# The x transposes of the expert two ahead, between up and the next gate

## The chip, the cores and the metric

The kernel runs on one core of a Trainium2 chip. The metric is the device time of one execution in microseconds. TensorE does the matmuls, VectorE and ScalarE take their results out of PSUM, GpSimd issues gathers, and SyncE issues the loads of the weights. Each engine works through its own queue in order, and semaphores are all that binds them.

## The reference

One step of a hybrid backbone over 128 context and 256 latent tokens, all in float32, with a model width of 1024: modulated norms, four token mixers, and then a mixture of 16 experts of width 512, two per token. The change lies in the last part alone:

```python
h = jax.nn.silu(jnp.einsum("td,edf->tef", t, w_gate)) * jnp.einsum("td,edf->tef", t, w_up)
h = h * gates.astype(h.dtype)[..., None]
return jnp.einsum("tef,efd->td", h, w_down).reshape(B, L, D)
```

## The kernel before

The expert stage takes experts one after another, in pairs (p is 0 or 1); all pairs but the first and the last run in a hardware loop. For each expert, GpSimd gathers its rows of the normed tokens (at most 96) into `xe`. TensorE turns them in eight transposes (`turn_x`, line 845, called by `load_x`) into PSUM banks 0 and 1, and ScalarE copies them to `xeT` (`xt_out`, line 1398). `gate` and `up` are eight terms each over 128 rows of contraction. They are packed: `packed` (lines 834 and 837) splits the array into four groups of 32 columns, of which three hold the 96 tokens' first 384 output columns and the fourth the other 128 for each of the three. A float32 term shows as two passes in the trace, each of three matmuls of 384 columns and three of 128, so `gate` is 16 passes, and `up` too. ScalarE applies silu to gate's result (`gate_silu`, line 1406, into `he`), and VectorE multiplies by up's (line 2011). TensorE transposes h (`turn_h`, three full transposes, line 851), VectorE copies these to `heT` (line 2015), and `down` multiplies by the third weight in the same packed form, again 16 passes. ScalarE and VectorE copy the two halves of the result and ScalarE's queue writes them out.

Nothing but the order of the code sets the order on an engine. TensorE's for expert n is: up of n; gate of n + 1; the h transposes of n; the x transposes of n + 2; down of n. The last pair has no x transposes. The weights lie in six slots, three for each parity; SyncE reloads a gate, up or down slot once that step of the expert in it is done, so each load is asked for nearly two expert steps before its use. The gather for expert n + 2 waits for the x transposes of expert n (`xt_filled`).

Of the kernel before, what the change touches and what calls it, by code (L numbers as in the profile page):

```python
# [154 lines left out]
def backbone_step(nc, cols, A, O):  # L155
# [10 lines left out]
    with ctx:  # L166
# [250 lines left out]
        def _(pe):  # L417
# [408 lines left out]
            n = len(uses)  # L826
# [3 lines left out]
            def packed(bank, x, w, terms):  # L830

                for k in range(terms):
                    for g in range(3):
                        mm(psum[32 * g:32 * g + 32, bank, 0:PACK], x(k, g), w(k)[:, 0:PACK], start=(k == 0),  # L834
                           stop=(k == terms - 1), tile_position=(0, 32 * g))
                    for g in range(3):
                        last = mm(psum[96:128, bank, tile(g)], x(k, g), w(k)[:, PACK:CW], start=(k == 0 and g == 0),  # L837
                                  stop=(k == terms - 1), skip_group_check=True, tile_position=(0, 96))
                return last

            def turn_x(src):

                for kt in range(KT):
                    c = kt % 4 * ROWS
                    last = tr(psum[:, kt // 4, c:c + ROWS], src[0:ROWS, tile(kt)], ident[0:ROWS, 0:ROWS])  # L845
                return last

            def turn_h(p):

                for q in range(3):  # L850
                    last = tr(psum[:, 4, tile(q)], he[:, p, tile(q)], ident)  # L851
                return last

            def up(p, bank, w):
                return packed(bank, lambda k, g: xeT[p][:, k, 32 * g:32 * g + 32], lambda k: w[:, k, :], KT)

            def down(half, w):
                return packed(5 + half, lambda q, g: heT[:, q, 32 * g:32 * g + 32] if q < 3 else heT[:, g, ROWS:P],
                              lambda q: w[:, q, half * CW:half * CW + CW], FE // P)

            def load_x(n, p, it):

                pe.wait_ge(s[f"xe{p}"], 16 * it + 16)
                turn_x(xe[p]).then_inc(s["xt_filled"], 1)

            def gate(n, p, it):

                pe.wait_ge(s["xt_ready"], n + 1)
                pe.wait_ge(loaded[NS * p], 16 * (it + (0 if p else PRE_USES)) + 16)
                up(p, 2, slot[NS * p]).then_inc(s["gate_done"], 1)  # L870

            def experts(it, first, last_pair):
                for p in range(2):
                    n = 2 * it + p
                    base = 0 if p else PRE_USES
                    pe.wait_ge(loaded[NS * p + 1], 16 * (it + base) + 16)
                    if not (first and p == 0):
                        pe.wait_ge(s["h_ready"], n)
                    up(p, 3, slot[NS * p + 1]).then_inc(s["up_done"], 1)
                    if not (last_pair and p == 1):  # L880
                        pe.wait_ge(s["g_silu"], n + 1)
                        gate(n + 1, 1 - p, it + p)
                    pe.wait_ge(s["h_ready"], n + 1)
                    if not (first and p == 0):
                        pe.wait_ge(s["ht_ready"], n)
                    turn_h(p).then_inc(s["ht_filled"], 1)
                    if not last_pair:
                        load_x(n + 2, p, it + 1)
                    w = slot[NS * p + 2][:, :, :].rearrange("p k n -> p (k n)").rearrange("p (k d) -> p k d", d=D)
                    pe.wait_ge(loaded[NS * p + 2], 16 * (it + base) + 16)  # L890
                    pe.wait_ge(s["ht_ready"], n + 1)
                    if not (first and p == 0):
                        pe.wait_ge(s["ya"], n)
                        pe.wait_ge(s["yb"], n)
                    down(0, w)
                    down(1, w).then_inc(s["down_done"], 1)
# [3 lines left out]
            load_x(1, 1, 0)  # L900
            gate(0, 0, 0)
            experts(0, True, False)
            with pe.Fori(1, E // 2 - 1) as it:
                experts(it, False, False)
            experts(E // 2 - 1, False, True)


# [227 lines left out]
        def _(act):  # L1135
# [249 lines left out]
            def write_rows(block, p, signal):  # L1385

                rows = A["y_rows"][block * ROWS:(block + 1) * ROWS, :] if isinstance(block, int) else \
                    A["y_rows"][bass.ds(block * ROWS, ROWS), :]
                act.dma_start(rows.rearrange("r (h c) -> r h c", h=2)[:, :, 0:PACK], yp[p][0:ROWS, :, :]
                              ).then_inc(signal, 16)  # L1390
                act.dma_start(rows.rearrange("(g r) (h c) -> r h g c", g=3, h=2)[:, :, :, PACK:CW],
                              yp[p][ROWS:P, :, :].rearrange("r h (g c) -> r h g c", g=3)).then_inc(signal, 16)

            def xt_out(n, p, reused):
                act.wait_ge(s["xt_filled"], n + 1)
                if reused:
                    act.wait_ge(s["up_done"], n - 1)
                a(xeTa[:, p].rearrange("p (b k) n -> p b (k n)", b=2), psum[:, 0:2, 0:KT // 2 * ROWS], ACT.Copy  # L1398
                  ).then_inc(s["xt_ready"], 1)

            def gate_silu(n, p, reused):

                act.wait_ge(s["gate_done"], n + 1)
                if reused:
                    act.wait_ge(s["ht_filled"], n - 1)
                a(he[:, p, 0:PACK], psum[:, 2, 0:PACK], ACT.Silu).then_inc(s["g_silu"], 1)  # L1406

            def experts(it, first, last_pair):
                for p in range(2):
                    n = 2 * it + p  # L1410
                    if not (last_pair and p == 1):
                        gate_silu(n + 1, 1 - p, not (first and p == 0))
                    if not last_pair:
                        xt_out(n + 2, p, True)
                    act.wait_ge(s["down_done"], n + 1)
                    if not first:
                        act.wait_ge(s[f"y_out{p}"], 32 * it)
                    a(yp[p][:, 0, :], psum[:, 5, 0:PACK], ACT.Copy).then_inc(s["ya"], 1)  # L1418
                    act.wait_ge(s["ya"], n + 1)
                    act.wait_ge(s["yb"], n + 1)  # L1420
                    write_rows(n, p, s[f"y_out{p}"])

            xt_out(0, 0, False)
            xt_out(1, 1, False)
            gate_silu(0, 0, False)
            experts(0, True, False)
            with act.Fori(1, E // 2 - 1) as it:
                experts(it, False, False)
            experts(E // 2 - 1, False, True)
            with act.If(further(act) > 0):  # L1430
                with act.Fori(0, OVER) as o:
# [655 lines left out]
```

## Time and profile before

| | us |
|---|---|
| median of 3 runs | 700.31 (699.57 to 706.39) |
| profiled execution, its own time | 701.97 |
| its span, first to last instruction | 700.0 |
| ten expert steps, 458.20 to 629.20 | 171.00 |
| TensorE busy in the span | 601.7 (86%) |

The expert stage begins at 385 us with the first x transposes and ends near 666 us. Mean granted clock of TensorE over the span is 0.939 of 2.4 GHz. A row of the timeline gives the start, the time from the first start to the last end of a group of like instructions, the engine and the line; PE is TensorE's matmuls and PEld its weight loads. Ends of matmuls are modelled.

### The profile page before, as it was taken

To read this page: it belongs to the slowest core of one execution; us is meant where nothing else is said; L and a number is where in the kernel's file an instruction comes from. 1 tells how busy PE (TensorE), PEld (TensorE's weight loads), DVE (VectorE), ACT (ScalarE), POOL (GpSimd) and SP (SyncE) were. 2 spreads that over 40 slices of the span, in tenths; PEclk is the share of its full clock that TensorE was granted. 3 is DMA by queue.
4 is the path that set the end of the run, shared out by engine and by line. 5 is a ranking of instruction groups with operands and counts; after the bars stand their busy time and mean duration, and the time that the engine had idled before them with its cause. 6 is when DMAs were issued, how large, how long until landed. Compare 5 with 4: busy or idle time off the path is not lost.

```text
span 700.0 us, 15233 instructions
## 1 busy us (share of the span) xinstructions
PE 601.7 (86%) x6792; PEld 473.6 (68%) x6792; DVE 252.2 (36%) x518; ACT 142.6 (20%) x254; POOL 61.3 (9%) x89
## 2 busy tenths in 40 slices
PE   2989999999998996799642999999999999999900
PEld 0665534666756565744342899999999999999800
DVE  2660768878648147110656300000000000011026
ACT  1421454322176110100240111111111111111012
POOL 1065000000110000200001100000000000200030
PEclk9999999999998999999875799999999999999965
DMA  8999330330305639960493499999999999999263
GB/s 260 384 356 326 114 120 0 121 118 3 120 8 185 236 108 371 319 151 0 177 413 131 150 356 395 391 392 393 400 391 399 394 395 394 400 408 411 105 198 127
DMA packets 80793, 177.15 MB, mean 253 GB/s; under 512 B 5992, under 2 KB 12911, under 8 KB 80367
## 3 DMA queue, kind: packets, MB, share of 16 engines
q1 hardware_dynamic: 64848, 149.01, 57.3%
q0 software_dynamic: 5728, 17.96, 7.8%
q10 hardware_dynamic: 10175, 9.56, 4.2%
q8 instruction: 32, 0.52, 0.3%
q14 instruction: 10, 0.08, 0.0%
HBM read 164.06 MB, written 12.47 MB: 252 GB/s over the span
## 4 chain that ended last, share of the span: by engine, by line
PE 49%; DVE 3%; issue 3%; DMA 3%; ACT 1%; POOL 1%; DVEq 0%; POOLq 0%; ACTq 0%
PE psum L837 20%; PE psum L834 16%; PE psum L770 5%; PE psum L845 2%; DMA slot<-in_w_out 2%; PE psum L777 2%; PE psum L851 1%; DVE SEL L1975 1%; POOL slot L1128 1%; PE psum L429 1%; DMA xe<-h_rows,lst 1%; PE psum L783 1%; DMA y_rows<-ye 1%; PE psum L810 0%; DVE XS L1900 0%
## 5 line engine op out<-in xcount | busy, mean ns | idle before, releaser
L837 PE MATMUL psum<-slot,xeTa 128*32 128x128 f32 x1536 | 172.2, 274 | 0.0
L834 PE MATMUL psum<-slot,xeTa 128*32 128x384 f32 x1536 | 170.3, 490 | 0.0
L837 PEld LDWEIGHTS psum<-slot,xeTa 128*32 128x32 f32 x1536 | 168.8, 111 | 0.4
L516 PE MATMUL psum<-hT,slot 128*128 128x384 f32 x304 | 100.8, 489 | 0.0
L834 PE MATMUL psum<-slot,heT 128*32 128x384 f32 x768 | 85.8, 487 | 1.9 <-issue 1.4
L837 PE MATMUL psum<-slot,heT 128*32 128x128 f32 x768 | 86.8, 273 | 0.0
L516 PEld LDWEIGHTS psum<-hT,slot 128*128 128x128 f32 x304 | 56.9, 190 | 38.2
L837 PEld LDWEIGHTS psum<-slot,heT 128*32 128x32 f32 x768 | 82.6, 110 | 0.0
L834 PEld LDWEIGHTS psum<-slot,xeTa 128*32 128x32 f32 x1536 | 68.9, 109 | 0.3 <-issue 0.2
L525 PE MATMUL psum<-slot,hT 128*128 128x512 f32 x96 | 42.3, 595 | 0.0
L2019 DVE COPY ye<-psum 128x384 f32<-128x384 f32 x16 | 8.9, 558 | 90.1 <-PE psum L837 90.1
L834 PEld LDWEIGHTS psum<-slot,heT 128*32 128x32 f32 x768 | 36.5, 109 | 4.5 <-issue 4.5
L1406 ACT ACTIVATE he<-psum 128x384 f32<-128x384 f32 x16 | 7.9, 491 | 154.5 <-PE psum L837 154.5
L2011 DVE TENSOR_TENSOR he<-he,psum 128x384 f32<-128x384 f32 x16 | 8.9, 555 | 80.1 <-PE psum L837 80.1
L2015 DVE COPY heT<-psum 128x384 f32<-128x384 f32 x16 | 8.9, 558 | 77.0 <-PE psum L851 77.0
L1107 POOL DMA_INDIRECT xe<-h_rows,lst x16 | 14.6, 914 | 218.5 <-PE psum L845 201.5
L525 PEld LDWEIGHTS psum<-slot,hT 128*128 128x128 f32 x96 | 18.0, 190 | 21.9 <-issue 21.6
L1032 POOL TENSOR_TENSOR stat<-stat,mhalf 128x3 f32<-128x3 f32 (+1 forms) x5 | 7.4, 1474 | 220.3 <-DVE stat L1740 128.6
L429 PE MATMUL psum<-slot,siluc 128*32 128x128 f32 x768 | 25.9, 294 | 0.0
L429 PEld LDWEIGHTS psum<-slot,siluc 128*32 128x32 f32 x768 | 22.4, 118 | 4.6 <-issue 4.0
L1418 ACT ACTIVATE ye<-psum 128x384 f32<-128x384 f32 x16 | 7.9, 492 | 83.7 <-PE psum L837 83.7
L1398 ACT ACTIVATE xeTa<-psum 128x768 f32<-128x768 f32 x16 | 13.0, 812 | 35.9 <-PE psum L845 35.9
(377 smaller groups left out, 717.8 us busy)
## 6 DMA issues: line engine op xcount, KB each, us to landing
slot<-in_w_gate SPq DMA_DIRECT2D x16, 2048.0 KB, 18.3
slot<-in_w_up SPq DMA_DIRECT2D x16, 2048.0 KB, 18.4
slot<-in_w_down SPq DMA_DIRECT2D x16, 2048.0 KB, 18.5
slot<-in_w_ada SPq DMA_DIRECT2D x12, 2048.0 KB, 13.2
slot<-in_w_in SPq DMA_DIRECT2D x7, 2048.0 KB, 8.9
y_rows<-ye ACTq DMA_DIRECT2D x16, 288.0 KB, 6.4
slot<-in_w_out SPq DMA_DIRECT2D x2, 2048.0 KB, 8.3
y_rows<-T POOLq DMA_DIRECT2D x7, 384.0 KB, 13.0
```

What stands on the lines that cost most here:

```text
L429: last = mm(o[32 * g:32 * g + 32, 0:P], siluc[:, kt, :], w[:, kt, tile(g)], start=(kt == 0), stop=(kt == KT - 1), tile_position=(0, 32 * g))
L516: last = mm(o[:, 0:TOK], w[:, kt, tile(i)], hT[:, kt, :], start=(kt == 0), stop=(kt == KT - 1))
L525: last = mm(o[:, :], hT[:, kt, tile(j)], w[:, kt, :], start=(kt == 0), stop=(kt == KT - 1))
L770: mm(banks[j, n][:, :], mixed[kt][:, tile(j)], w[n][:, kt, :], start=(kt == 0), stop=False)
L777: last = mm(banks[j, n][:, :], mixed[kt][:, tile(j)], w[n][:, kt, :], start=False, stop=(kt == KT - 1))
L834: mm(psum[32 * g:32 * g + 32, bank, 0:PACK], x(k, g), w(k)[:, 0:PACK], start=(k == 0), stop=(k == terms - 1), tile_position=(0, 32 * g))
L837: last = mm(psum[96:128, bank, tile(g)], x(k, g), w(k)[:, PACK:CW], start=(k == 0 and g == 0), stop=(k == terms - 1), skip_group_check=Tru ...
L845: last = tr(psum[:, kt // 4, c:c + ROWS], src[0:ROWS, tile(kt)], ident[0:ROWS, 0:ROWS])
L1107: g.indirect_dma_start(out=xe[n % 2][0:ROWS, :], out_offset=None, in_=A["h2_rows"], in_offset=bass.IndirectOffsetOnAxis(ap=lst[0:ROWS, n:n ...
L1398: a(xeTa[:, p].rearrange("p (b k) n -> p b (k n)", b=2), psum[:, 0:2, 0:KT // 2 * ROWS], ACT.Copy).then_inc(s["xt_ready"], 1)
L2011: v.tensor_tensor(he[:, p, 0:PACK], he[:, p, 0:PACK], psum[:, 3, 0:PACK], ALU.mult).then_inc(s["h_ready"], 1)
L2015: v.tensor_copy(heT[:, :, :].rearrange("p q n -> p (q n)"), psum[:, 4, 0:PACK]).then_inc(s["ht_ready"], 1)
```

## The change

`load_x` for expert n + 2 moves from behind `turn_h` to behind `up`, ahead of the next `gate`. It gets a wait for `xt_ready`, that the copy of the expert before out of banks 0 and 1 is done; `gate` waits for the same value. On ScalarE the copy to `xeT` moves ahead of the silu, so that its queue keeps the order in which TensorE makes the two.

```diff
@@ TensorE
                     up(p, 3, slot[NS * p + 1]).then_inc(s["up_done"], 1)
+                    if not last_pair:
+                        pe.wait_ge(s["xt_ready"], n + 2)
+                        load_x(n + 2, p, it + 1)
                     if not (last_pair and p == 1):
                         pe.wait_ge(s["g_silu"], n + 1)
                         gate(n + 1, 1 - p, it + p)
@@
                     turn_h(p).then_inc(s["ht_filled"], 1)
-                    if not last_pair:
-                        load_x(n + 2, p, it + 1)
@@ ScalarE
                     n = 2 * it + p
+                    if not last_pair:
+                        xt_out(n + 2, p, True)
                     if not (last_pair and p == 1):
                         gate_silu(n + 1, 1 - p, not (first and p == 0))
-                    if not last_pair:
-                        xt_out(n + 2, p, True)
```

TensorE's queue before, in expert 0's step, at the border of its up (slot 1) and the gate of expert 1 (slot 3):

```order
L834 MATMUL psum<-slot1,xeTa 32x384 x3
L837 MATMUL psum<-slot1,xeTa 32x128 x3
L834 MATMUL psum<-slot3,xeTa 32x384 [waits loaded3,xt_ready,g_silu]
L834 MATMUL psum<-slot3,xeTa 32x384 x2
L837 MATMUL psum<-slot3,xeTa 32x128 x3
```

and after, at the same border:

```order
L834 MATMUL psum<-slot1,xeTa 32x384 x3
L837 MATMUL psum<-slot1,xeTa 32x128 x3
L845 MATMUL psum<-const,xe0 128x96 [waits xe0,xt_ready]
L845 MATMUL psum<-const,xe0 128x96 x7
L834 MATMUL psum<-slot3,xeTa 32x384 [waits loaded3,xt_ready,g_silu]
L834 MATMUL psum<-slot3,xeTa 32x384 x2
L837 MATMUL psum<-slot3,xeTa 32x128 x3
```

Eight transposes, their wait for the gathered rows and one for `xt_ready` have come in between.

TensorE's queue before, later in the same step, from the end of that gate to the start of down (slot 2):

```order
L837 MATMUL psum<-slot3,xeTa 32x128 x3
L851 MATMUL psum<-const,he 128x128 [waits h_ready]
L851 MATMUL psum<-const,he 128x128 x2
L845 MATMUL psum<-const,xe0 128x96 [waits xe0]
L845 MATMUL psum<-const,xe0 128x96 x7
L834 MATMUL psum<-slot2,heT 32x384 [waits ht_ready,loaded2]
```

and after:

```order
L837 MATMUL psum<-slot3,xeTa 32x128 x3
L851 MATMUL psum<-const,he 128x128 [waits h_ready]
L851 MATMUL psum<-const,he 128x128 x2
L834 MATMUL psum<-slot2,heT 32x384 [waits ht_ready,loaded2]
L834 MATMUL psum<-slot2,heT 32x384 x2
```

Down's first matmul, with its wait for VectorE's copy of heT, now stands directly behind the h transposes.

## Rows read from the trace of the kernel before

**Rows 1.** The page's part 2: 40 slices of 17.5 us, in tenths.

```profile
PE   2989999999998996799642999999999999999900
...
PEclk9999999999998999999875799999999999999965
```

**Rows 2.** Busy time by stretches: ten expert steps.

```profile
458.20:629.20 171.00, 170.66 (x2991) 167.13 (x2991) 16.70 (x30) 17.95 (x30) 11.00 (x14) 1.00 1.04 396
```

**Rows 3.** Waits, 440 to 645 us: total, times, longest.

```profile
POOL xe L1107 <- PE psum L845: 161.9, 10, 16.2
...
PEld psum L834 <- issue: 2.3, 12, 0.2
```

**Rows 4.** Timeline, TensorE, expert 6, gate's end to down's start.

```profile
509.49 0.31 PEld L851 LDWEIGHTS psum<-const,he 128*128 128x128 f32 x3 [0.20 <-issue]
...
509.77 0.75 PEld L845 LDWEIGHTS psum<-const,xe 96*128 96x128 f32 x8
509.87 0.83 PE L845 MATMUL psum<-const,xe 96*128 96x96 f32 x8
...
510.70 0.15 PEld L834 LDWEIGHTS psum<-slot,heT 128*32 128x32 f32 x4 [0.19 <-issue]
```

**Rows 5.** Timeline, VectorE: experts 0 and 6.

```profile
401.78 0.56 DVE L2011 TENSOR_TENSOR he<-he,psum 128x384 f32<-128x384 f32 x1 [9.52 <-PE psum L837]
...
504.43 0.56 DVE L2011 TENSOR_TENSOR he<-he,psum 128x384 f32<-128x384 f32 x1 [4.75 <-PE psum L837]
510.07 0.56 DVE L2015 COPY heT<-psum 128x384 f32<-128x384 f32 x1 [5.09 <-PE psum L851]
```

**Rows 6.** Timeline, TensorE's weight loads and VectorE, expert 14 (no x transposes).

```profile
646.30 0.31 PEld L851 LDWEIGHTS psum<-const,he 128*128 128x128 f32 x3 [0.20 <-issue]
...
646.89 0.56 DVE L2015 COPY heT<-psum 128x384 f32<-128x384 f32 x1 [5.09 <-PE psum L851]
...
647.51 0.15 PEld L834 LDWEIGHTS psum<-slot,heT 128*32 128x32 f32 x4 [0.90 <-issue]
```

**Rows 7.** Timeline, TensorE's weight loads, expert 0.

```profile
406.84 0.31 PEld L851 LDWEIGHTS psum<-const,he 128*128 128x128 f32 x3 [0.20 <-issue]
407.12 0.75 PEld L845 LDWEIGHTS psum<-const,xe 96*128 96x128 f32 x8
408.10 0.15 PEld L834 LDWEIGHTS psum<-slot,heT 128*32 128x32 f32 x4 [0.23 <-issue]
```

**Rows 8.** Timeline, TensorE's matmuls, expert 6, where up meets gate.

```profile
504.27 0.53 PE L834 MATMUL psum<-slot,xeTa 128*32 128x384 f32 x3
...
504.60 0.53 PE L834 MATMUL psum<-slot,xeTa 128*32 128x384 f32 x3
```

**Rows 9.** Timeline, TensorE's matmuls, expert 7, gate's last passes.

```profile
525.57 0.53 PE L834 MATMUL psum<-slot,xeTa 128*32 128x384 f32 x3
...
525.89 0.53 PE L834 MATMUL psum<-slot,xeTa 128*32 128x384 f32 x3
...
526.59 0.55 PE L851 MATMUL psum<-const,he 128*128 128x128 f32 x3
```

**Rows 10.** Timeline, TensorE, ahead of the expert stage: full transposes, then packed matmuls.

```profile
284.31 0.30 PEld L437 LDWEIGHTS psum<-const,modrow 128*128 128x128 f32 x2 [0.20 <-issue]
284.31 0.39 PE L437 MATMUL psum<-const,modrow 128*128 128x8 f32 x2
284.63 0.48 PEld L429 LDWEIGHTS psum<-slot,siluc 128*32 128x32 f32 x19
```

**Rows 11.** DMA issues, 440 to 630 us: count, KB, median us to landing.

```profile
slot<-in_w_gate SPq DMA_DIRECT2D x11, 2048.0 KB, 19.2
...
xe<-h_rows,lst POOLq DMA_INDIRECT x10, 7.4
```

**Rows 12.** Timeline, TensorE's matmuls, gate of expert 0, first two passes.

```profile
389.12 0.86 PE L834 MATMUL psum<-slot,xeTa 128*32 128x384 f32 x3
...
389.76 0.86 PE L834 MATMUL psum<-slot,xeTa 128*32 128x384 f32 x3
```

## The prediction

> **What bounds the kernel now.** I read the page's slices first. From about 400 to 665 us TensorE's row shows 9 in every slice and the other engines 0 to 3; the granted clock is 9 there as well [rows 1]. The stage streams expert weights all the while, at 396 GB/s and a share of 1.04 of the DMA engines [rows 2]. So two things could set the pace of the expert stage, the matmuls or the weight stream, and the change is worth something only by which of them it is. The view of busy time by stretches settles half of it, with the same row: the ten expert steps from 458.20 to 629.20 us take 171.00 us, 17.10 each, TensorE is busy for 170.66 of them, at the full clock of 2.4 GHz (1.00) [rows 2]. The view of waits settles the other half. In 440 to 645 us no TensorE row waits for a DMA, only for "issue", 0.2 us at a time, while GpSimd waits for TensorE up to 16.2 us at a time [rows 3]; the rows of ScalarE and VectorE name TensorE too. The stage is a chain of TensorE steps, one expert after another. A microsecond put on TensorE's queue in an expert step is a microsecond of the result, unless it fills one of the few gaps. So the question is which gap the eight x transposes (L845) fill now, and which they will fill.
>
> **Now: they fill a gap.** The timeline at the end of expert 6's step shows the order [rows 4]: the weight loads of the three h transposes (L851) begin at 509.49, those of the x transposes at 509.77, and the first of `down` (L834, heT) at 510.70. `down` can't start before VectorE has copied heT out of PSUM. That copy (L2015) runs from 510.07 for 0.56 us, to 510.63 [rows 5], and `down` starts 0.07 later. From the first L851 to `down` it is 1.21 us. Experts 14 and 15 have no x transposes, since no expert follows by two. There L851 begins at 646.30, the copy runs from 646.89 to 647.45, and `down` begins at 647.51: 1.21 us again, with 0.90 us of it put down as "issue" in place of 0.19 [rows 6]. So the x transposes are free today. They lie wholly in the time in which TensorE waits for the copy.
>
> **Part 1, taking them out of that place.** `down` then starts where it starts in expert 14, 1.21 us behind L851. The gain is 0, at most the 0.05 us by which expert 0, whose x transposes begin at 407.12 behind L851 at 406.84, was later (`down` at 408.10, 1.26 us) [rows 7]. What is late next is the copy, and nothing covers it any more.
>
> **Part 2, putting them between up and gate.** Today that place has no gap at all: `up` ends and `gate` begins inside one stream of passes 0.32 to 0.33 us apart, with no idle time in the rows (504.27, 504.60 [rows 8]; the border lies there, since VectorE takes up's product at 504.43 [rows 5]). Three things are paid there.
>
> Entering: where packed matmuls (four column groups of 32) give way to full-array transposes, at the gate to L851 border, the last packed pass starts at 525.89 and L851 at 526.59: 0.70 us, where the next pass of the stream came 0.32 us after the one before (525.57 to 525.89) [rows 9]. The surplus is 0.38 us. `up` has the same form as `gate`, so I take the same 0.38.
>
> The transposes: their weight loads span 0.75 us, their matmuls from 509.87 to 510.70, or 0.93 us behind the first load [rows 4].
>
> Leaving: no place in the stage shows it clean, since the copy ends last there. The nearest rows are earlier in the kernel, where two full-array transposes (L437) are followed by packed adaLN matmuls (L429): the packed load starts at 284.63, 0.02 us behind the last load's end (284.61) and 0.07 us ahead of the modelled end of the matmuls (284.31 + 0.39 = 284.70) [rows 10]. So I take 0.93 - 0.07 = 0.86 us from the first x load to gate's first. The bounds are 0.75 + 0.02 = 0.77, if only the loads count, and 408.10 - 407.12 = 0.98, as in expert 0 [rows 7].
>
> The sum for one expert is 0.38 + 0.86 = 1.24 us, between 1.15 and 1.36. The moved call runs for experts 0 to 13, since the last pair leaves it out: 14 times. 14 x 1.24 = 17.4 us, between 16.1 and 19.0. All of it lies on the path: 0 us of it is given back in part 1.
>
> The Trainium skill, page "TensorEngine Tiling (Array Packing)", section "Key Properties", speaks against the change: changing the tiling mode drains TensorE, and the change adds two such borders to each expert and takes none away. By that rule, taken for both borders to the matmuls' modelled end, the sum would be 14 x (0.38 + 0.93) = 18.3 us; the trace agrees at the entering border (0.38 us) and shows 0.07 us less than the whole at the leaving one.
>
> **Part 3, waits and queues.** The new wait of TensorE on xt_ready asks for the copy of the expert before, a whole step old, and `gate` asked for the same one. The wait on xe moves 5 to 6 us earlier in the step. The gather for it is issued right behind the transposes of two steps before, which GpSimd waits for [rows 3], and lands in 7.4 us [rows 11], so it is there some 25 us ahead. At the first two calls the margin is smallest: the gathers for experts 2 and 3 go out behind the two leading groups of transposes, about when gate's first pass starts at 389.12 [rows 12], so they land by about 398. The new place is reached when expert 0's up ends, near 401.8, at which time VectorE takes its product [rows 5]. GpSimd's queue sees the same steps. On ScalarE the xeTa copy (L1398, 0.81 us) now comes ahead of the silu (L1406): it is released when `gate` begins and `gate` takes 16 passes, 5.2 us, so the silu isn't held up. The weight loads wait for the ends of gate, up and down and take 19.2 us to land [rows 11]: the slot that a gate frees near 509.5 is full near 528.7 and used near 538.5 (504.27 + 2 x 17.10), 9 us spare, and the longer step adds to that.
>
> Against the profiled execution (701.97 us, span 700.0) this gives 719.4 us; the median of the three runs is 1.66 us lower, 700.31, and the forecast goes by it: 700.31 + 17.4 = 717.7 us.
>
> **The rivals.** (a) The border is cheap: up's last packed passes and the first transposes overlap, and only the 0.83 us of the transposes' matmuls count. 14 x 0.83 = 11.6, that is 711.9 us. For it speaks that L851 shows only 0.20 us of idle in its row; against it the 0.70 us between starts. (b) Not slower: the weight stream, not TensorE, sets the pace, the loads fill the DMA engines (396 GB/s, share 1.04 [rows 2]) and 1.24 us more on TensorE fit in front of weights that are late anyway. It decides if the slots are full less than 1.24 us before use. Then the time stays at 700.3. Against it speak the 9 us of margin and the absence of any DMA among TensorE's releasers. (c) Faster: the x transposes hold `down` back, in place of the copy. They end, by the model, at 510.70, the very time at which `down` starts. Were they the last, freeing `down` would gain up to 0.9 us in each expert, and if up to gate took them for less, the kernel would be faster; at most 14 x 0.07 = 1 us is left by the copy's end, so at best 699. Experts 14 and 15 refute it. (d) The clock: TensorE's granted clock falls after the new break. At the lower level of 1.2 GHz passes start 0.64 us apart (389.12 to 389.76 [rows 12]), so eight slow passes would add 2.6 us to each expert, 36 us in all, 754. The 0.90 us idle in expert 14 is a break of the same kind, and there is nothing of that in the rows behind it. The Trainium skill ("TensorE: Matmul & The Clock Gate", section "Part 4: PE-mode transpose") says that transposes don't count as TensorE being busy for the clock, which would speak for (d); the transposes here stand inside stretches at 1.00.
>
> **How the numbers follow.** Forecast 0.85; (a) 0.09; (b) 0.02; (c) 0.01; (d) or a late gather 0.03. A measurement of this kernel tells about 1% (7 us) from no change. Faster by over 1%: 0.01, since (c) has hardly a way to reach it. Within 1%: 0.03, (b) and the rest of (c). Slower: 0.96. The range goes from 711.5, which takes in (a), to 722: 19.0 us above the median is 719.3, and the three runs lie up to a few us above their middle.
>
> **What would show it.** In the profile of the changed kernel the step from L851 to L851 is 18.3 us, in place of 17.10; L851 to `down` stays at 1.21 us, with 0.9 us of "issue" in every expert; the first x load comes 0.70 us behind up's last pass, and gate's first load 0.86 us behind it; heT's copy is unmoved against L851; the DMA rate falls to about 370 GB/s. I am wrong if `down` starts earlier behind L851 than the copy's end, if gate's first pass starts much less than 1.5 us behind up's last, if TensorE shows a wait for xe or a slot, or if the clock falls below 1.00 between 420 and 660 us.

## The result and the profile after

The changed kernel takes 713.47 us (median of 4 runs, 708.85 to 714.89) against 699.94 for the kernel before: a ratio of 1.0169, interval 1.0099 to 1.0238. Timed again in more rounds it is 712.67 against 700.26, ratio 1.0179, interval 1.0150 to 1.0208, which is 10.5 to 14.6 us. It is slower, as forecast (717.7, range 711.5 to 722.0), by about 4 to 5 us less than forecast.

The two profiled executions stand 10.6 us apart (712.59 and 701.97). That is not the change alone: gate's first pass lies at 386.63 here and at 389.12 before [rows 12], so the part ahead of the experts, where the code is the same, came out 2.5 us shorter in this execution. In the profiled executions below that part is between 384.7 and 393.2 us long, so a single time says little about a change of a few us. The steps are compared below, not the spans.

The page's slices, TensorE and its granted clock, answer to [rows 1]:

```profile
PE   2889999999989996899534999999999999999800
...
PEclk9999999999999998899865999999999999999965
```

The expert stage is still a row of nines at the full clock. Busy time by stretches, ten steps from one first h transpose to another (columns: stretch, length, busy PE, PEld, DVE, ACT, POOL, granted clock, DMA share, GB/s), beside [rows 2]:

```profile
459.68:640.18 180.50, 173.53 (x2991) 166.35 (x2990) 16.69 (x30) 17.91 (x30) 10.06 (x13) 1.00 1.04 396
```

180.50 us for ten steps is 18.05 each, where it was 17.10. TensorE is busy for 173.5 of them, so 7.0 us are idle now, 0.7 in each step, where 0.3 in ten steps were. The view of waits, 440 to 645 us, says where they stand, beside [rows 3]:

```profile
PEld psum L834 <- issue: 10.9, 12, 0.9
PE psum L834 <- issue: 8.4, 12, 0.7
```

The weight loads of `down` stand idle 0.9 us twelve times in that window (2.3 us in all before). No transfer is named as a releaser of TensorE. The timeline of TensorE and VectorE in expert 6's step (lines of the changed kernel: the copy of heT is L2016), beside [rows 4], [rows 5], [rows 8] and [rows 9]:

```profile
507.02 0.53 PE L834 MATMUL psum<-slot,xeTa 128*32 128x384 f32 x3
507.12 0.60 PE L837 MATMUL psum<-slot,xeTa 128*32 128x128 f32 x4
507.64 0.70 PEld L845 LDWEIGHTS psum<-const,xe 96*128 96x128 f32 x8 [0.20 <-issue]
...
508.46 0.12 PEld L834 LDWEIGHTS psum<-slot,xeTa 128*32 128x32 f32 x3
...
508.81 0.50 PE L834 MATMUL psum<-slot,xeTa 128*32 128x384 f32 x3
508.83 0.49 PE L837 MATMUL psum<-slot,xeTa 128*32 128x128 f32 x3
...
513.32 0.50 PE L834 MATMUL psum<-slot,xeTa 128*32 128x384 f32 x3
513.41 0.49 PE L837 MATMUL psum<-slot,xeTa 128*32 128x128 f32 x3
...
513.84 0.31 PEld L851 LDWEIGHTS psum<-const,he 128*128 128x128 f32 x3 [0.20 <-issue]
...
514.42 0.56 DVE L2016 COPY heT<-psum 128x384 f32<-128x384 f32 x1 [6.04 <-PE psum L851]
...
515.05 0.15 PEld L834 LDWEIGHTS psum<-slot,heT 128*32 128x32 f32 x4 [0.91 <-issue]
```

Read from the bottom: L851 to `down` is 1.21 us, as in expert 14 of the kernel before [rows 6], and the copy's end (514.98) is 0.07 ahead of it. Read from the top: up's last pass to the first x load is 0.62 us, that is 0.30 over a pass; the first x load to gate's first is 0.82 us; and gate's last pass to L851 is 0.52 us, 0.20 over a pass, where it was 0.70 and 0.38 [rows 9]. The step's growth is 0.82 + 0.30 + 0.20 - 0.38 = 0.94 us, which is the 0.95 measured. The moved call stands in 14 experts: 13.3 us.

So one term of my sum is off: entering costs a step 0.12 net (0.30 + 0.20 - 0.38), not 0.38, because the border further on became cheaper. That had to be explained, and the other steps checked by themselves.

### The profile page after: what moved, and what is told of

It is laid out like the page before. It is cut to its first block, busy times and chain, and to the rows that moved or that the text cites. A ratio compares the mean times of both kernels' runs of the same rounds, so it can differ in the third digit from the quotient of the medians.

```text
span 710.8 us, 15253 instructions
## 1 busy us (share of the span) xinstructions
PE 603.7 (85%) x6792; PEld 470.9 (66%) x6792; DVE 251.9 (35%) x518; ACT 142.5 (20%) x254; POOL 61.1 (9%) x89
## 4 chain that ended last, share of the span: by engine, by line
PE 49%; issue 4%; DVE 3%; DMA 3%; ACT 1%; POOL 1%; DVEq 0%; POOLq 0%; ACTq 0%
PE psum L837 22%; PE psum L834 15%; PE psum L770 5%; PE psum L845 2%; DMA slot<-in_w_out 2%; PE psum L777 1%; PE psum L851 1%; DVE SEL L1976 1%; POOL slot L1129 1%; PE psum L429 1%; PE psum L783 1%; DMA xe<-h_rows,lst 1%; DMA y_rows<-ye 0%; PE psum L810 0%; DVE XS L1901 0%
## 5 line engine op out<-in xcount | busy, mean ns | idle before, releaser
L837 PE MATMUL psum<-slot,xeTa 128*32 128x128 f32 x1536 | 175.0, 275 | 0.0
L834 PE MATMUL psum<-slot,xeTa 128*32 128x384 f32 x1536 | 173.3, 491 | 0.0
L837 PEld LDWEIGHTS psum<-slot,xeTa 128*32 128x32 f32 x1536 | 167.8, 111 | 0.5
L834 PE MATMUL psum<-slot,heT 128*32 128x384 f32 x768 | 85.8, 487 | 11.2 <-issue 10.5
L837 PE MATMUL psum<-slot,heT 128*32 128x128 f32 x768 | 86.8, 273 | 0.0
L837 PEld LDWEIGHTS psum<-slot,heT 128*32 128x32 f32 x768 | 82.5, 110 | 0.0
L834 PEld LDWEIGHTS psum<-slot,xeTa 128*32 128x32 f32 x1536 | 65.3, 110 | 1.9 <-issue 0.2
L834 PEld LDWEIGHTS psum<-slot,heT 128*32 128x32 f32 x768 | 36.4, 110 | 14.5 <-issue 14.5
L2016 DVE COPY heT<-psum 128x384 f32<-128x384 f32 x16 | 8.9, 558 | 90.3 <-PE psum L851 90.3
L1108 POOL DMA_INDIRECT xe<-h_rows,lst x16 | 14.6, 912 | 223.5 <-PE psum L845 206.6
L429 PE MATMUL psum<-slot,siluc 128*32 128x128 f32 x768 | 26.2, 295 | 0.0
```

The lines of the kernel that those rows point to most:

```text
L429: last = mm(o[32 * g:32 * g + 32, 0:P], siluc[:, kt, :], w[:, kt, tile(g)], start=(kt == 0), stop=(kt == KT - 1), tile_position=(0, 32 * g))
L1108: g.indirect_dma_start(out=xe[n % 2][0:ROWS, :], out_offset=None, in_=A["h2_rows"], in_offset=bass.IndirectOffsetOnAxis(ap=lst[0:ROWS, n:n ...
L2016: v.tensor_copy(heT[:, :, :].rearrange("p q n -> p (q n)"), psum[:, 4, 0:PACK]).then_inc(s["ht_ready"], 1)
```

## The experiments

Theory A: a packed run falls behind. The fourth column group does three matmuls (L837) for the one that each other group does in a pass (L834), and each of them costs a few ns of its own. The group falls behind pass by pass, and a full-array step behind the run waits for the pile. A break in the run lets it catch up. The rows above show the lag: L837 starts 0.02 us behind L834 in gate's second pass (508.83, 508.81) and 0.09 behind in the last (513.41, 513.32): 0.07 us in 14 passes, 5 ns each. Theory B: the drain (the wait for the packed matmuls to be done) is fixed, and the gate runs quicker behind x for another reason.

The Trainium skill ("TensorE: Matmul & The Clock Gate", section "Wait — 56ns, not 53.3ns?") states a fixed cost of about 2.5 ns for each warm matmul. Two matmuls more in a pass would be 5 ns, an estimate from that figure, and the trace agrees.

The rows also show what the full-array step waits for. Behind 48 passes, in expert 7 of the kernel before, the fourth group's last row is

```profile
525.95 0.71 PE L837 MATMUL psum<-slot,xeTa 128*32 128x128 f32 x5
```

It has five matmuls where a pass has three, so it also holds two of the pass before, and it ends at 526.66 by the model; L851 is at 526.59 [rows 9], 0.07 ahead of that end. Behind 32 passes (507.12 + 0.60 = 507.72) the x load is 0.08 ahead of it, behind 16 (513.41 + 0.49 = 513.90) L851 is 0.06 ahead. The lag changes, and the distance from the end of the group that ends last doesn't: it is 0.07 us at this border in every kernel profiled here.

It follows that the lag is paid by the passes, however they are divided. From a run's first packed matmul to the next full-array load it is 5.38 us for 16 passes (508.46 to 513.84), 10.61 for 32 (497.03 to 507.64) and 15.86 for 48 (510.73 to 526.59): 5.24 us for each 16 passes, and 0.14 once for each run. A break that makes two runs of one adds one such 0.14. This is the net price of entering; the 0.12 above is the same, by rounded rows and the passes' starts.

**The fourth group cut short, in the old and in the moved order**

Eight of each 128 columns of the fourth group are left out.

```diff
-                        last = mm(psum[96:128, bank, tile(g)], x(k, g), w(k)[:, PACK:CW], start=...
+                        last = mm(psum[96:128, bank, g * P:g * P + 120], x(k, g), w(k)[:, PACK:PACK + 120], start=...
```

> The kernel before, with the fourth column group's matmuls (line 837) cut from 128 to 120 columns: 8 of 512 output columns of each packed product of each third of the tokens are left out. Theory A (lag): the fourth group does three matmuls where the others do one, falls behind by some 5 to 6 ns in each pass, and a full-array step behind packed matmuls has to wait for what has been piled up: 0.38 us of surplus after 48 passes in a row, 0.30 after 32, 0.20 after 16, so a fixed part of about 0.12 and the rest lag. With a shorter fourth group the lag can't arise: surplus from gate's last pass to the h transposes about 0.12, step 16.83 us in place of 17.10, time some 4 us lower than before (16 steps). Theory B (fixed drain, and the moved kernel's gate is quicker for another reason): the surplus stays 0.38 and the step 17.10, time as before.

> The changed kernel with the same cut (8 of each 128 columns of the fourth group left out). Theory A: both surpluses (up to x, gate to h) fall to about 0.12, step 18.05 - 0.27 = 17.78 us, and the price of the move over the cut kernel in the old order is 0.12 + 0.82 = 0.94 us a step. Theory B: step 18.05, both surpluses as in the changed kernel (0.30 and 0.20).

Measured in the old order: the nine heT copies from 478.80 to 613.64 are 16.86 us apart, so 0.24 us a step less. 697.69 us against 699.89, ratio 0.9961 (0.9931 to 0.9990). Its TensorE rows at one gate's end:

```profile
511.14 0.85 PE L834 MATMUL psum<-slot,xeTa 128*32 128x384 f32 x6
...
511.93 0.55 PE L851 MATMUL psum<-const,he 128*128 128x128 f32 x3
```

The first row holds two passes, the last of them at 511.14 + 0.32 = 511.46; L851 follows 0.47 us behind it, 0.15 over a pass in place of 0.38. In the moved order the step is 17.80 us (17.78 expected), 0.25 less than 18.05, with up's last pass to x and gate's last to L851:

```profile
494.20 0.53 PE L834 MATMUL psum<-slot,xeTa 128*32 128x384 f32 x3
494.65 0.88 PE L845 MATMUL psum<-const,xe 96*128 96x96 f32 x8
...
500.33 0.49 PE L834 MATMUL psum<-slot,xeTa 128*32 128x384 f32 x2
...
500.75 0.55 PE L851 MATMUL psum<-const,he 128*128 128x128 f32 x3
```

0.45 and 0.42 us, 0.13 and 0.10 over a pass. The time is 709.42, ratio 1.0122 (1.0092 to 1.0152). Theory B expected no change in either. What is left over, 0.10 to 0.15 us, is the fixed part of a border. Here the other three groups end last, and the next step is again 0.06 to 0.08 us ahead of their modelled end (511.99 and 511.93; 494.73 and 494.65; 500.82 and 500.75). Between the two cut kernels the move costs 17.80 - 16.86 = 0.94 us a step, the expected 0.94, and as much as the 0.95 with the lag: the lag is no part of the price of the move.

The old order's cut kernel gained 2.7 us by its ratio (0.7 to 4.8 by the interval), where 0.24 us times 16 is 3.9. The interval takes in both, but its waits, 386 to 690 us, show something that the kernel before doesn't:

```profile
PEld psum L834 <- DMA slot<-in_w_down: 1.2, 2, 0.9
PEld psum L834 <- DMA slot<-in_w_up: 0.8, 2, 0.6
...
PEld psum L834 <- DMA slot<-in_w_gate: 0.4, 1, 0.4
```

TensorE waits for weights, 2.4 us in these three rows. So the weight stream is near the pace of the old order, which the section on the prediction takes up.

**The break in another place**

The x transposes go between `down` and the next `up`:

```diff
-                    if not last_pair:
-                        load_x(n + 2, p, it + 1)
...
                     down(1, w).then_inc(s["down_done"], 1)
+                    if not last_pair:
+                        pe.wait_ge(s["xt_ready"], n + 2)
+                        load_x(n + 2, p, it + 1)
```

> The changed kernel with the x transposes between down and the next up, so that 16 packed passes stand ahead of them and 32 ahead of the h transposes, the mirror image of the changed kernel. Theory A (lag by run length): last pass to x load 0.52 us, last pass of gate to L851 0.63 us, step 18.05 as in the changed kernel. Theory B (the place in the step, not the length of the run, sets it: behind up 0.63, behind gate 0.52): gate to L851 stays 0.52 us. Theory C (fixed drain): both 0.70, step 18.3.

The step is 18.05 us (heT copies at 479.06 and 497.10, 515.16 and 533.20), the time 714.71. TensorE's matmuls ahead of x (behind 16 passes) and ahead of the h transposes (behind 32):

```profile
502.63 0.49 PE L834 MATMUL psum<-slot,heT 128*32 128x384 f32 x2
502.72 0.49 PE L837 MATMUL psum<-slot,heT 128*32 128x128 f32 x3
503.14 0.88 PE L845 MATMUL psum<-const,xe 96*128 96x96 f32 x8
...
513.97 0.50 PE L834 MATMUL psum<-slot,xeTa 128*32 128x384 f32 x3
514.04 0.60 PE L837 MATMUL psum<-slot,xeTa 128*32 128x128 f32 x4
514.57 0.55 PE L851 MATMUL psum<-const,he 128*128 128x128 f32 x3
```

The first row is the second part of a pass that begins at 502.60, so x follows 0.54 us behind the last pass; gate to L851 is 0.60. The changed kernel has 0.62 behind 32 passes and 0.52 behind 16. So the longer wait has moved with the longer run, but each is 0.02 to 0.03 us off what theory A expected (0.52 and 0.63); why the last pass starts that much earlier or later isn't shown. The fourth group accounts for it: it ends at 503.21 and 514.64 by the model, 0.07 us behind the next full-array step in both places. It is the length of the run, not the place, that sets the wait. Theory A stands; both forms of the fixed drain (0.52 behind gate as in the changed kernel, or 0.70 at both borders and a step of 18.3) fall.

**One x transpose of eight, in the old and in the new place**

```diff
-                        load_x(n + 2, p, it + 1)
+                        load_x(n + 2, p, it + 1, [0])
```

(`turn_x` takes the list of the column tiles that it turns.)

> The kernel before, with one x transpose of eight for the experts from 2 on (seven eighths of their tokens' transpose are left out). Theory A (the x transposes lie wholly under VectorE's copy of heT): L851 to down stays 1.21 us, step 17.10, time as before. Rival (the x transposes hold down back): L851 to down falls to some 0.6 us, or by up to 0.07 if both end together, step down to 16.5 or 17.03.

> The changed kernel with one x transpose of eight in the new place for the experts from 2 on. Theory A: a transpose costs its pitch of 0.083 us, so the first x load to gate's first load is 0.82 - 7 x 0.083 = 0.24 us, the border 0.13 more; step 17.10 + 0.37 = 17.47 us, time 5.2 us above before. Rival (the border is what costs, by a fixed drain of 0.38 and more): step 17.8 or above.

Old place: the step is 17.10 us and the time 699.61, against 700 with eight. Weight loads of one step:

```profile
507.51 0.31 PEld L851 LDWEIGHTS psum<-const,he 128*128 128x128 f32 x3 [0.20 <-issue]
507.79 0.14 PEld L845 LDWEIGHTS psum<-const,xe 96*128 96x128 f32 x1
508.73 0.15 PEld L834 LDWEIGHTS psum<-slot,heT 128*32 128x32 f32 x4 [0.80 <-issue]
```

`down` starts at the same distance, 1.22 us, with seven transposes less. The x transposes were free, and rival (c) is refuted by a run. New place: the step is 17.47 us, as expected to the last digit shown, and the time 704.39. So the other seven cost 0.58 us there, 0.083 each, and 0.37 us come with the first: 0.23 for that transpose and its leaving border, and 0.14 for the entering one, net.

**Sixteen x transposes in the old place**

```diff
-                        load_x(n + 2, p, it + 1)
+                        load_x(n + 2, p, it + 1, list(range(KT)) * 2)
```

> The kernel before with each x transpose of the loop done twice (16 in the old place). Theory A: the cover ends where the x transposes end by 1.21 us behind L851; sixteen of them end 0.60 us later, so L851 to down is 1.81 us and step 17.70; time 8.4 us above before. Rival (wider cover): less than 0.3 more.

The step is 17.66 us and the time 705.82 (700.30 for the kernel before on the same chip). That is 5.5 us more, where 8.4 were expected and 14 steps of 0.56 are 7.8; each is a single run.

```profile
509.26 0.31 PEld L851 LDWEIGHTS psum<-const,he 128*128 128x128 f32 x3 [0.20 <-issue]
509.54 1.41 PEld L845 LDWEIGHTS psum<-const,xe 96*128 96x128 f32 x16
511.06 0.12 PEld L834 LDWEIGHTS psum<-slot,heT 128*32 128x32 f32 x3
```

Weight loads again: L851 to `down` is 1.80 us, 0.59 more, but the step grew by 0.56. With eight transposes `down`'s weight load (510.70 [rows 4]) stands 0.03 us ahead of its first matmul (510.73), with sixteen the two start together, at 511.06; matmul to matmul it is 1.24 and 1.80 us, the 0.56 of the step. Eight more transposes of 0.083 us are 0.67, so 0.11 us were still free under the copy, a little over one transpose. The cover ends at nine.

**The x transposes ahead of the h transposes**

```diff
+                    if not last_pair:
+                        load_x(n + 2, p, it + 1)
                     pe.wait_ge(s["h_ready"], n + 1)
...
                     turn_h(p).then_inc(s["ht_filled"], 1)
-                    if not last_pair:
-                        load_x(n + 2, p, it + 1)
```

> The kernel before with the eight x transposes ahead of the three h transposes in place of behind them: no packed border is added, but the copy of heT covers nothing. Theory A: step is 17.10 plus eight pitches, 0.67 to 0.75, 17.8 us; time some 10 us above before; the rest of the 0.95 of the changed kernel (0.2 to 0.28) is the price of the added border. Rival (the new border is most of the loss and the lost cover little): step under 17.4.

The step is 17.76 us, the time 711.65. With no border added, the lost cover alone costs 0.66 us, eight times 0.083. The other 0.29 of the changed kernel's 0.95 are the two added borders: 0.14 for entering, and 0.15 for leaving (0.81 us from the first x matmul to gate's first, 507.65 to 508.46, less 0.66).

**ScalarE's order alone**

```diff
-                    if not last_pair:
-                        xt_out(n + 2, p, True)
                     if not (last_pair and p == 1):
                         gate_silu(n + 1, 1 - p, not (first and p == 0))
+                    if not last_pair:
+                        xt_out(n + 2, p, True)
```

> The changed kernel with ScalarE's old order (silu ahead of the xeTa copy), TensorE's order as changed. Every theory: the order on ScalarE is off the path, step 18.05 us, time within 0.3% of the changed kernel. If ScalarE's new order cost or gained something, the step differs.

The step is 18.05 us and the time 714.63, 0.3% above the changed kernel's median in one run. The order on ScalarE does nothing.

**The changed kernel again**

> The changed kernel itself, timed in more rounds against the kernel before, to narrow the interval of 1.010 to 1.024. By the steps of the profile (18.05 against 17.10 us, 14 times) it is 13.3 us, a ratio of 1.019.

712.67 us against 700.26, ratio 1.0179 (1.0150 to 1.0208); 1.019 is inside.

**Both groups of transposes in the middle of gate**

The copy of heT needs some 0.9 us of cover, and x is not the only thing that could give it.

```diff
-            def packed(bank, x, w, terms):
+            def packed(bank, x, w, terms, middle=None):
                 for k in range(terms):
+                    if middle and k == terms // 2:
+                        middle()
...
-                        gate(n + 1, 1 - p, it + p)
-                    pe.wait_ge(s["h_ready"], n + 1)
...
+                        gate(n + 1, 1 - p, it + p, turns)
```

(`turns` holds the wait for h, `turn_h` and `load_x`, as they stood behind gate.)

> The kernel before with the three h transposes and the eight x transposes together in the middle of the next gate, behind four of its eight terms, so that gate's other half covers the copy of heT. Theory A: one full-array group a step as before, at 0.38 us of surplus plus 1.10 us (three and eight transposes), where L851 to down is 1.21 us before: step 16.99 in place of 17.10, and 0.7 us less for expert 14, so 2 us in all, if the weights are there. The landing time of the weights, which grows from 14 to 25 us along the stage before, then decides the rest: where the loads come late by the last experts, the gain is 0 to 2 us (0.3% at most, as the cut kernel in the old order lost part of its gain to waits for weights). Rival (the split gate costs a border more than it saves): slower by 14 x 0.2 = 3 us.

697.61 us against 700.26, ratio 0.9955 (0.9929 to 0.9982): faster than both kernels. Weight loads in the middle of a gate, with L853 and L847 for the h and the x transposes and L836 for the packed matmuls, then ten steps by stretches:

```profile
502.96 0.31 PEld L853 LDWEIGHTS psum<-const,he 128*128 128x128 f32 x3 [0.20 <-issue]
503.24 0.75 PEld L847 LDWEIGHTS psum<-const,xe 96*128 96x128 f32 x8
504.10 0.12 PEld L836 LDWEIGHTS psum<-slot,xeTa 128*32 128x32 f32 x3
```

```profile
452.56:622.54 169.98, 169.98 (x2993) 166.85 (x2992) 16.69 (x31) 16.82 (x30) 10.94 (x14) 1.00 1.04 396
```

The packed matmuls go on 1.14 us behind L853, where `down` had to wait for 1.21. The step is 17.00 us, the run between two breaks still 48 passes, and TensorE has no idle time in it. 14 times 0.10 and 0.7 for expert 14 make 2.1 us; the medians are 2.65 us apart, with an interval of 1.3 to 5.0. No wait for weights shows.

## Why the prediction was right, and where it was off

The measured time lies in the range, but below what my sum allowed. The sum's own bounds, 16.1 to 19.0 us, give 716.4 to 719.3; the steps show 13.3 us. The range reached down to 711.5 only to take in rival (a). So the direction, the free old place and the path were right by reasoning, and that the size fell in the range is partly luck.

**TensorE sets the pace: right.** 18.05 times 10 with no transfer among TensorE's releasers, and each experiment's step came within 0.04 us of what was expected by theory A. But my argument against rival (b), 9 us of margin for a weight slot, was too easy. I took one median. By stretch, the landing time of gate's weights grows: 16.0 us from 440 to 480 and 22.9 from 560 to 600 in the kernel before, 11.8 and 10.3 in the changed one. DMA issues, kernel before, then changed, 560 to 600 us:

```profile
slot<-in_w_gate SPq DMA_DIRECT2D x3, 2048.0 KB, 22.9
```

```profile
slot<-in_w_gate SPq DMA_DIRECT2D x2, 2048.0 KB, 10.3
```

The rate is 396 GB/s in both, and didn't fall to 370, as I had written. Three weights, the gather and the result are 3 x 2.10 + 2 x 0.39 = 7.08 MB, which at 396 GB/s is 17.9 us. So the stream needs 17.9 us for a step; at 17.10 it falls behind and lives on the slots that were full at the start, and at 18.05 it keeps up. The cut kernels bear this out: at 17.80 the landing time of gate's weights grows by only 1.5 us from the load at 429.9 (13.1) to that at 590.0 (14.6), at 16.86 by 11 us from that at 427.9 (15.0) to that at 598.9 (26.2). With slots freed 29 us ahead of their use, some 4 to 6 us of margin were left by the last experts of the kernel before, and none in the cut kernel at 16.86. The change was still paid in full. With more experts in the stage the kernel before would have met this limit and the loss would have shrunk; that is argued, no run has more experts.

**The old place was free: right.** One transpose in it or eight, 17.10 us. L851 to `down` stays at 1.21 us behind the change.

**Entering, 0.38: the step that failed.** The gap of 0.70 us at gate's end was read rightly, and `up` has the same form, but the gap belongs to the length of the run ahead of it: 48 passes there, and 32 ahead of x. I also left out that the break shortens the run ahead of L851 to 16. Some 0.24 us of the 0.38 is the lag of 48 passes, which the step pays with the break and without it; only the fixed part, 0.12 to 0.14 us, was added. That is 3.4 to 3.6 us of the 4.1 by which 17.4 exceeds 13.3, and the next term is the rest. The first sign that I had named showed it: gate's first load came 507.02 to 508.46, 1.44 us, behind up's last pass, not 1.56.

**The transposes and leaving, 0.86 (0.77 to 0.98): 0.82.** The loads spanned 0.70 us in place of 0.75. Where packed loads follow full-array ones, they started before the modelled end of the matmuls, as [rows 10] had it: 507.65 + 0.88 = 508.53, and the load at 508.46, 0.07 ahead.

By the rule of the Trainium skill that changing the tiling mode drains TensorE ("TensorEngine Tiling (Array Packing)", section "Key Properties") both borders would have cost their drain, 18.3 us in all. The trace agrees with the rule in kind: each border waits for the group that ends last, but for 0.07 us, and x ahead of h, with no border added, costs 0.66 where the changed kernel costs 0.95. It doesn't with the size that I gave it.

**Waits and queues: right.** No wait for xe or a slot in the steps, and ScalarE's order makes no difference. **The clock, rival (d):** 1.00 in the ten steps, with transposes between packed runs and 0.9 us of idle time in each step. Its price of eight slow passes came from no row. **Rival (a)** gave 711.9 and lies closer to what was measured than the forecast, by 11.6 for 13.3 us, but not for its reason: the transposes overlapped with up's last matmuls by no more than 0.08 us, and what made entering cheap is that its lag was paid already.

## What to carry to other kernels

An instruction that stands between a transpose and the step that waits for its copy may be free there and cost its whole time anywhere else. Look for the idle time that would stand there without it, in a step of the same kernel that lacks it, as experts 14 and 15 did. Before a gap is charged to a kind of border, ask what led up to it: where parallel groups of matmuls are unevenly loaded, the gap holds what they piled up. And a margin of a transfer is a trend along a stage, not a median.

## What the runs showed of the hardware

A packed run of four column groups, of which one does three matmuls of 128 columns in place of one of 384, falls behind by about 5 ns a pass: the next full-array load came 0.20, 0.30 and 0.38 us later than a pass would after 16, 32 and 48 passes (0.22 and 0.28 after 16 and 32 with the breaks elsewhere), and 0.10 to 0.15 us with the three cut to 120 columns. Where no semaphore holds it back, the first full-array load begins 0.06 to 0.08 us ahead of the modelled end of the last packed matmul, whichever group that is in, and in the other direction packed loads begin 0.07 us ahead of the modelled end of the last full-array matmul. A run of packed passes pays 0.14 us once for being a run of its own, and a group of transposes between two runs 0.15 us more. Transposes of 96 x 128 in float32 follow each other by 0.083 us.
